# Expert blocks in 512-column products: even and odd parts of the model dimension in the four column groups, summed after the turn

## What is computed

```python
def swiglu(x, wg, wu, wd):
    return (jax.nn.silu(x @ wg) * (x @ wu)) @ wd

out = swiglu(xt, s_gate, s_up, s_down)
for e in range(N_EXPERTS):          # 16 experts, each token uses two
    out = out + gates[:, e:e + 1] * swiglu(xt, w_gate[e], w_up[e], w_down[e])
```

## Time and profile before

| | |
|---|---|
| three runs | 2373.59, 2375.11, 2384.86 us |
| span of the profiled execution | 2369.5 us |
| PE busy | 1976.5 us (83%) |
| DVE, ACT, POOL busy | 951.9, 701.9, 331.0 us |
| expert blocks of layer 0 | about 774 to 1127 us of the span |
| expert blocks of layer 1 | about 2060 to 2346 us |

### The profile page before, as it was taken

How to read it: one execution, slowest core, us unless ns; L and a number is a source line. 1 busy time by engine, 2 the same in 40 slices (tenths; PEclk the granted TensorE clock), 3 DMA queues, 4 the chain that set the end, 5 groups by cost and what they waited for, 6 DMA issues and landing times. The chain is left out here.

```text
span 2369.5 us, 58411 instructions
## 1 busy us (share of the span) xinstructions
PE 1976.5 (83%) x26021; PEld 1357.2 (57%) x26021; DVE 951.9 (40%) x1675; ACT 701.9 (30%) x1524; POOL 331.0 (14%) x211
## 2 busy tenths in 40 slices
PE   6999998998989788889396897678888887967775
PEld 3777765446744344445243783678888855634333
DVE  3184244783051111111434774666676552211112
ACT  3234543763230000000314223545544222000001
POOL 1443400003310000000110541311122000000000
PEclk8999998998989899989698997899999978988888
DMA  8544525004374897977520300000000025999984
GB/s 301 196 178 167 189 107 200 14 1 142 108 274 165 312 340 269 343 250 273 164 97 27 107 27 1 3 4 4 4 4 4 4 92 173 323 381 348 343 316 177
DMA packets 184017, 381.14 MB, mean 161 GB/s; under 512 B 14394, under 2 KB 43670, under 8 KB 183510
## 3 DMA queue, kind: packets, MB, share of 16 engines
q1 hardware_dynamic: 165216, 343.82, 40.7%
q10 hardware_dynamic: 15094, 20.99, 2.9%
q0 software_dynamic: 3456, 12.58, 1.4%
HBM read 634.54 MB, written 25.95 MB: 279 GB/s over the span
## 5 line engine op out<-in xcount | busy, mean ns | idle before, releaser
L1810 PE MATMUL banks<-arena 128*32 128x256 f32 x1696 | 234.1, 424 | 94.6 <-DMA arena<-in_exp_w_up_dram 94.6
L369 PE MATMUL banks<-parts 128*128 128x512 f32 (+1 forms) x1096 | 243.9, 375 | 22.1 <-DVE parts L383 11.3
L1811 PE MATMUL banks<-arena 128*32 128x256 f32 x1696 | 234.1, 424 | 0.0
L369 PEld LDWEIGHTS banks<-parts 128*128 128x128 f32 x1096 | 195.2, 193 | 59.4 <-DVE parts L383 11.5
L1810 PEld LDWEIGHTS banks<-arena 128*32 128x32 f32 x1696 | 105.5, 120 | 184.4 <-DMA arena<-in_exp_w_up_dram 102.9
L377 DVE TENSOR_TENSOR arena<-banks,arena 64x256 f32<-64x256 f32 (+3 forms) x128 | 65.5, 512 | 339.3 <-ACT arena L1876 244.5
L2559 PE MATMUL banks<-arena 64*64 64x64 f32 x4224 | 159.5, 225 | 49.5 <-DVE arena L380 19.2
L1876 ACT ACTIVATE arena<-banks 64x256 f32<-64x256 f32 x78 | 29.7, 381 | 573.3 <-PE banks L1811 573.3
L2559 PEld LDWEIGHTS banks<-arena 64*64 64x64 f32 x4224 | 148.2, 140 | 53.0 <-DVE arena L380 20.5
L2559 PE MATMUL banks<-ring 64*64 64x64 f32 x4224 | 159.2, 225 | 8.0 <-issue 7.8
L369 PE MATMUL banks<-arena,ring 128*128 128x256 f32 (+1 forms) x528 | 156.5, 459 | 8.5 <-PEq L316 8.5
(11 more groups left out here) (368 smaller groups left out, 3601.9 us busy)
## 6 DMA issues: line engine op xcount, KB each, us to landing
arena<-in_exp_w_gate_dram SPq DMA_DIRECT2D x106, 1024.0 KB
arena<-in_exp_w_up_dram SPq DMA_DIRECT2D x106, 1024.0 KB
arena<-in_exp_w_down_dram SPq DMA_DIRECT2D x53, 2048.0 KB
ring<-in_exp_w_gate_dram SPq DMA_DIRECT2D x50, 1024.0 KB
ring<-in_exp_w_up_dram SPq DMA_DIRECT2D x50, 1024.0 KB
ring<-in_exp_w_down_dram SPq DMA_DIRECT2D x25, 2048.0 KB
ring<-in_w_mod_dram SPq DMA_DIRECT2D x24, 2048.0 KB, 9.1
ring<-in_ab_w_in_dram SPq DMA_DIRECT2D x10, 2048.0 KB, 13.9
```

The lines of the kernel that those rows point to most:

```text
L369: m = nc.tensor.matmul(o, a, b, start=first and n == 0, stop=last and n == len(pairs) - 1)
L1810: nc.tensor.matmul(o[r:r + BLOCK, 0:256], x, up[:, k, c], start=k == 0, stop=k == KD - 1)
L1811: m = nc.tensor.matmul(o[64 + r:64 + r + BLOCK, 0:256], x, gate[:, k, c], start=k == 0, stop=k == KD - 1)
```

## The change

`gate_up` now takes the slices of the model dimension in pairs. The four column groups hold up with the even slice, up with the odd slice, gate with the even slice and gate with the odd slice, each over all 512 columns. So PSUM holds two partial sums for up and for gate, 128 x 512 in all. ScalarE copies this to SBUF (`m_raw`), TensorE turns it in four transpositions of 128 x 128 (`turn_gate_up`), and VectorE sums even and odd parts while it reads the turned values (`tensor_reduce`). ScalarE applies Silu to the gate's sums, and VectorE multiplies. `down` likewise holds even and odd slices for two halves of 512 output columns; ScalarE copies the odd rows and VectorE adds them. The loads of the weights, and their conditions, stay; "first half" is now ticked at the end of the second pair, behind the turn.

```diff
-                        turn_hidden(i - 1)
+                        turn_gate_up(i - 1)
                     if i < nb:
-                        gate_up(i, 1)
+                        for pair in range(1, 4):
+                            gate_up(i, pair)
...
-                pe.wait_ge(half_landed[part][p], 32 * (w0[p] + i // 3 + 1))
-                if part == 0:
+                if pair % 2 == 0:
+                    pe.wait_ge(half_landed[pair // 2][p], 32 * (w0[p] + i // 3 + 1))
+                if pair == 0:
...
-                for k in range(4 * part, 4 * part + 4):
-                    x = m_xt[:, g % 2, k, BLOCK * (i % 2):BLOCK * (i % 2) + BLOCK]
-                    for half in range(2):
-                        c, r = slice(256 * half, 256 * half + 256), BLOCK * half
-                        nc.tensor.matmul(o[r:r + BLOCK, 0:256], x, up[:, k, c], start=k == 0, stop=k == KD - 1)
-                        m = nc.tensor.matmul(o[64 + r:64 + r + BLOCK, 0:256], x, gate[:, k, c], start=k == 0, stop=k == KD - 1)
+                for first_row, w in ((0, up), (64, gate)):
+                    for odd in range(2):
+                        k, r = 2 * pair + odd, first_row + BLOCK * odd
+                        x = m_xt[:, g % 2, k, BLOCK * (i % 2):BLOCK * (i % 2) + BLOCK]
+                        m = nc.tensor.matmul(o[r:r + BLOCK, :], x, w[:, k, :], start=pair == 0, stop=pair == 3)
...
+            def turn_gate_up(i):
+                pe.wait_ge(*at(("rows out", i)))
...
+                pe.wait_ge(*at(("sums", i - 1)))
+                for c in range(4):
+                    m = nc.tensor.transpose(ps[2][:, c * P:(c + 1) * P], m_raw[:, c * P:(c + 1) * P], ident[:])
...
+                for pair in range(2):
+                    for odd in range(2):
+                        for half in range(2):
+                            k, r = 2 * pair + odd, 64 * odd + BLOCK * half
+                            m = nc.tensor.matmul(ps[3 + i % 2][r:r + BLOCK, :], m_th[:, i % 2, k, :], w[:, k, 512 * half:512 * half + 512],
+                                                 start=pair == 0, stop=pair == 1)
...
                     if i >= 2:
                         store_y(i - 2)
+                    if 0 < i <= nb:
+                        act.wait_ge(*at(("sums", i - 1)))
+                        nc.scalar.activation(m_sums[:, :, 1, :], m_sums[:, :, 1, :], ACT.Silu).then_inc(act_done, act.tick(("silu", i - 1)))
                     if i < nb:
                         act.wait_ge(*at(("gate up", i)))
-                        nc.scalar.activation(m_sil[0:64, :], ps[i % 2][64:P, 0:256], ACT.Silu).then_inc(act_done, act.tick(("silu", i)))
+                        nc.scalar.activation(m_raw, ps[i % 2], ACT.Copy).then_inc(act_done, act.tick(("rows out", i)))
...
+                    if 0 < i <= nb:
+                        act.wait_ge(*at(("down", i - 1)))
+                        act.wait_ge(*at(("y out", i - 2)))
+                        nc.scalar.activation(m_odd[0:64, :], ps[3 + (i - 1) % 2][64:P, :], ACT.Copy).then_inc(act_done, act.tick(("odd rows out", i - 1)))
...
+                turned = ps[2].rearrange("p (s o t) -> p s t o", s=8, o=2)
+                for i in range(1, nb + 1):
+                    dve.wait_ge(*at(("gate up turned", i - 1)))
+                    dve.step(nc.vector.tensor_reduce(m_sums.rearrange("p c s t -> p (c s) t"), turned, AX.X, ALU.add), ("sums", i - 1))
+                    dve.wait_ge(*at(("silu", i - 1)))
+                    dve.wait_ge(*at(("down", i - 3)))
+                    vmul(m_th[:, (i - 1) % 2], m_sums[:, :, 0, :], m_sums[:, :, 1, :]).then_inc(dve_done, dve.tick(("hidden", i - 1)))
+                    dve.wait_ge(*at(("odd rows out", i - 1)))
...
+                    vadd(m_yout[0:64, (i - 1) % 2, :], ps[3 + (i - 1) % 2][0:64, :], m_odd[0:64, :]).then_inc(dve_done, dve.tick(("y out", i - 1)))
```

More of the change, by code:

```diff
@@ L1565, in program @@
         m_x = region(0, 2, D)
-        m_yout = region(2048, 2, 256)
-        m_sil, m_hid = region(3072, 256), region(3584, 256)
+        m_yout = region(2048, 2, 512)
+        m_raw, m_odd = region(3072, 512), region(3584, 512)
         m_squares = region(0, TT, D), region(14520, 2, D)
@@ L1574, in program @@
         m_xt = region(8560, 2, KD, 2 * BLOCK)
-        m_th = region(9584, 2, 2, 2 * BLOCK)
+        m_th = region(9584, 2, 4, BLOCK)
+        m_sums = region(9840, 4, 2, BLOCK)
         m_vtok = region(4096, TT, D)
@@ L1796, in turn_x, with gate_up @@
                 m.then_inc(pe_done, pe.tick(("x turned", g)))
-            def gate_up(i, part):
+            def gate_up(i, pair):
                 p, g, o = i % 3, i // 2, ps[i % 2]
-                pe.wait_ge(half_landed[part][p], 32 * (w0[p] + i // 3 + 1))
-                if part == 0:
+                if pair % 2 == 0:
+                    pe.wait_ge(half_landed[pair // 2][p], 32 * (w0[p] + i // 3 + 1))
+                if pair == 0:
                     pe.wait_ge(*at(("x out", g)))
-                    pe.wait_ge(*at(("hidden", i - 2)))
+                    pe.wait_ge(*at(("rows out", i - 2)))
@@ L1812, in gate_up @@
-                m.then_inc(pe_done, pe.tick(("gate up" if part else "first half", i)))
-            def turn_hidden(i):
-                pe.wait_ge(*at(("hidden", i)))
+                for first_row, w in ((0, up), (64, gate)):
[3 more added lines that the diff above has]
+                        m = nc.tensor.matmul(o[r:r + BLOCK, :], x, w[:, k, :], start=pair == 0, stop=pair == 3)
@@ L1816, in turn_hidden @@
+                if pair % 2:
+                    m.then_inc(pe_done, pe.tick(("gate up" if pair == 3 else "first half", i)))
+            def turn_gate_up(i):
+                pe.wait_ge(*at(("rows out", i)))
                 pe.wait_ge(*at(("shared out", 2 * nt - 1)))
[L1817 to L1820, removed]
+                pe.wait_ge(*at(("sums", i - 1)))
+                for c in range(4):
+                    m = nc.tensor.transpose(ps[2][:, c * P:(c + 1) * P], m_raw[:, c * P:(c + 1) * P], ident[:])
+                m.then_inc(pe_done, pe.tick(("gate up turned", i)))
@@ L1822, in down @@
             def down(i):
                 p = i % 3
-                pe.wait_ge(*at(("hidden out", i)))
+                pe.wait_ge(*at(("hidden", i)))
                 pe.wait_ge(*at(("y out", i - 2)))
@@ L1986, in dve_ @@
                     nc.vector.tensor_copy(m_ysh[:, d // 2, 512 * (d % 2):512 * (d % 2) + 512], ps[2 + d % 5]).then_inc(dve_done, dve.tick(("shared out", d)))
[L1987 to L2001, removed]
+                turned = ps[2].rearrange("p (s o t) -> p s t o", s=8, o=2)
[6 more added lines that the diff above has]
+                    dve.wait_ge(*at(("odd rows out", i - 1)))
+                    s = y0 + i - 1
+                    if i >= 3:
+                        dve.wait_ge(y_stored[s % 2], 16 * (s // 2))
+                    vadd(m_yout[0:64, (i - 1) % 2, :], ps[3 + (i - 1) % 2][0:64, :], m_odd[0:64, :]).then_inc(dve_done, dve.tick(("y out", i - 1)))
                 if l == 0:
```

3 lines of the change are left out of this document (1 added, 2 removed).

## The result

The changed kernel took 2467.37 us in the median of four runs (2463.02 to 2469.20), the kernel before 2374.45 us, now with a fourth run. The ratio is 1.0392, with a 95% interval of 1.0362 to 1.0421. The profiled span is 2467.3 us. The forecast was 2388.6 us: the sign was right, the size was not, by some 79 us, and the range did not hold the time.

What follows compares the result with a forecast made beforehand. Weight loads set the pace in some stretches, PE in 32 of 78 blocks. PE-bound blocks 9.6, layer ends 3.0 and 1.5, stores -0.6 sum to 13.5 us more: 2388.6 us, range 2375 to 2399 us.

Steps and rivals of the forecast that it cites:

- The DMA step: Stores of y: 64 packets of 2 KB replace 128 of 1 KB, gaining 0.6 us over some 46 DMA-bound stores.
- The sign: Whole kernel: slower by 0.57%, at 2388.6 us; slower had a chance of 0.52.
- the turn: On PE in each block: four transpositions and the switch take 0.73 us instead of 0.41, 0.32 us dearer.
- the ends: Behind each layer's last block nothing covers the chain: 3.0 us more in layer 1, 1.5 us in layer 0.
- A later release only shortens a backlog: Where the DMA share is 1.0, releasing the next weight loads later was costed at nothing.
- The products: On PE: 12 rounds of 512 columns at 0.428 us replace 24 of 0.216, gaining 0.03 us a block.
- The rival that wide products save a fixed cost: On PE: fewer rounds save 0.3 us a block, so PE-bound blocks break even: 2379 us; chance 0.10.
- The chain through three engines: Reduction, Silu and product before down: one microsecond of cover is left in the loop, so costed at nothing.
- the rival of an exposed chain: Reduction beyond 1.7 us makes PE wait in each PE-bound block; at 2.2 us the time is 2407 us; chance 0.12.
- The stages: Both layers' expert loops: 32 PE-bound blocks at 0.28 us more, plus 0.6 us for half-clock turns, 9.6 us.
- The end of layer 1: From the last turn to the gather: the longer chain adds 3.0 us, all on the path to the gather.
- Less is exposed: Rival: loads released early hide the turns in 19 blocks of layer 0, 5.3 us less, 2383 us; chance 0.28.

Runs made afterwards that it cites:

- the control: Kernel before with sixteen-engine stores, plus 128 KB of extra stores a block to contiguous unused DRAM, which ran on sixteen engines: 2342.52 us, ratio 0.9881.

## Why the prediction was wrong, point by point

**The DMA step failed.** It read "0.012 us a store over 16 engines" and put the change of the stores at a gain of 0.6 us. The packets' times were right, 45 and 87 ns, but nothing in the text had checked how many engines carried them. The store's pattern went from a first dimension of 4 to one of 2, and with it from four engines to two. In place of the gain of 0.6 us there was a loss of some 75 us: with the stores on two engines the unchanged compute takes 73 us more, and with the stores on sixteen the changed kernel takes 120 us less and lies at 0.989 of the kernel before. PE's waits for expert weights are 167 us with two engines, 83 with sixteen, and 116 in the kernel before with four. The clue was in the trace of before: behind a burst of loads the share stayed near 0.26 for microseconds, while PE went on. The same step had also missed that the kernel before was itself slower by 41 to 45 us than with stores on sixteen engines; some 37 us of that lie inside the two loops.

**The sign was luck.** The forecast said slower because of the turn and the ends. These are there, some 18 us. But four fifths of the loss come from a term that the prediction had with the other sign.

**"A later release only shortens a backlog" was not refuted.** Releasing the loads earlier gained nothing, in a kernel that was late by another cause.

**The products held.** Rounds of four 512-column products come at 0.43 us, half as many, for the same time. The rival that wide products save a fixed cost fell: a block would have stayed near 5.58 us, and it is 5.87 us. The Trainium skill (TensorEngine Tiling (Array Packing), section Instruction Overhead) gives each product some 60 cycles of overhead; the trace does not show them between the rounds.

**The turn held.** I had 5.85 us for a full-clock block, the trace has 5.87.

**The chain through three engines stayed hidden.** The reduction took 0.69 us, as costed, though it reads pairs 32 elements apart; the rival of an exposed chain fell. In the stretches with full-clock blocks `down` followed `gate_up` without a gap. With stores on sixteen engines `down` waited for VectorE once in each layer, 2.4 us, behind the last `gate_up`.

**The stages, on the two kernels with sixteen-engine stores.** Between the first and the last reading of `gate_up`'s result, layer 0 takes 337.7 us against 331.2 (6.5 more; I had 7.3), and layer 1 takes 259.7 against 255.0 (4.7 more; I had 2.2). From the last such reading to the gather, layer 0 takes 13.5 against 11.8 us (1.7 more; I had 1.5), and from it to the end of the span layer 1 takes 31.0 against 27.8 us (3.1 more; I had 3.0). That makes 16.0 us, against the 14.1 us of the sum without its DMA term. The two profiled spans are 19.8 us apart; the other 3.8 us are before the first block (1.2 less) and between the layers (5.0 more), in code that is the same in both, and I cannot say more of it than that it is of the size by which runs of the kernel before differ from each other.

**The end of layer 1 was longer than costed in the changed kernel itself.** From the last reading of `gate_up`'s result to the gather it took 15.6 us against 8.3, so 7.2 more in place of 3.0: 3.0 were `down` waiting for its weights, 1.9 the slower last store, and 2.3 are left for the longer chain.

**"Less is exposed" fell.** On the kernels with sixteen-engine stores this rival had 4.3 us for the loops and the forecast 9.6; the two loops show 11.2. In the changed kernel itself the waits for weights cover the question.

## What to carry to other kernels

Before pricing a DMA by bytes and packets, find out how many engines it uses: count its completions in the queue's packets, or read the share while it runs alone; a share of 0.125 or 0.25 in a quiet stretch means two or four of sixteen. Here small transfers on few engines delayed the large ones that were spread over all, and where there were many of them they also held up the engine that issued them. When a change of layout alters the first dimension of a store, it can alter this number; here, splitting the store so that each part has a first dimension of 32 rows brought it to sixteen. An experiment that adds DMAs should be read on the issuing engine too, and not only at the wait that it was made for.

## What the runs showed of the hardware that I had not expected

128 KB beside each block cost 12 to 16 us in all when spread over sixteen engines, and some 130 us on two. With them on two engines, a single DMA issue held ScalarE for up to 6.3 us, against 1.7 us in the control. A contiguous target let a DMA that was written with a first dimension of 2 run on sixteen engines (32 completions for two DMAs), while the same form with rows 4 KB apart kept two. The spread stores are four DMAs in place of one on ScalarE's queue, and no wait of PE shows them. Putting sixteen engines to the stores of the kernel before makes it 1.9% faster.
